# Hybrid diffusion backbone on one Trainium2 core: where the bias of the adaLN conditioning is added

## The reference, cut to what matters

```
mp = adaln(c_ctx[None, :], ada_w[l], ada_b[l])      # (silu(cond) @ w + b).reshape(6, D)
ms = adaln(c, ada_w[l], ada_b[l])
...
ap = modulate(rmsnorm(hp, norm1_g[l]), mp, 0)       # x * (1 + mod[1]) + mod[0]
...
hp = hp + mp[:, 2][:, None, :] * op                 # mod[2]: gate of the mixer
...
hp = hp + mp[:, 5][:, None, :] * hier_moe(modulate(rmsnorm(hp, norm2_g[l]), mp, 3), ...)
```

## Time and profile before

| what | value |
|---|---|
| median of 3 runs | 1781.94 us (1778.7, 1781.94, 1781.96) |
| the profiled execution, its own time | 1779.51 us |
| span of that execution (first to last instruction) | 1777.6 us |
| PE busy | 1667.9 us, 94% of the span |
| DVE, ACT, POOL busy | 606.5, 369.6, 100.1 us |
| DMA | 614.04 MB, mean 345 GB/s |
| line 741 (bias products), PE busy | 12.7 us in 384 records |

### The profile page before, as it was taken

How to read it: one execution, slowest core, us unless ns; L and a number is a source line. 1 busy time by engine, 2 the same in 40 slices (tenths; PEclk the granted TensorE clock), 3 DMA queues, 4 the chain that set the end, 5 groups by cost and what they waited for, 6 DMA issues and landing times.

```text
span 1777.6 us, 20153 instructions
## 1 busy us (share of the span) xinstructions
PE 1667.9 (94%) x8226; PEld 833.1 (47%) x8226; DVE 606.5 (34%) x1327; ACT 369.6 (21%) x705; POOL 100.1 (6%) x158
## 2 busy tenths in 40 slices
PE   5989999899999999899999999988999999999995
PEld 2443333376544333334864433335786654433331
DVE  1142323300532323130176232314333993423233
ACT  2031111110431111120202111112222662311111
POOL 0000000000000000000000000000001960000000
PEclk8999999999999999999999999999999999999998
DMA  9999999996769999998556999998864585899992
GB/s 391 376 423 425 427 425 425 405 365 241 290 243 426 425 426 427 423 373 341 204 194 254 425 425 426 427 423 318 308 237 168 127 268 209 317 418 424 426 425 115
DMA packets 98415, 614.04 MB, mean 345 GB/s; under 512 B 8112, under 2 KB 8384, under 8 KB 52112
## 3 DMA queue, kind: packets, MB, share of 16 engines
q1 hardware_dynamic: 91376, 585.73, 81.0%
q0 software_dynamic: 6944, 26.96, 4.6%
HBM read 608.34 MB, written 4.33 MB: 345 GB/s over the span
## 4 chain that ended last, share of the span: by engine, by line
PE 71%; DMA 14%; DVE 7%; ACT 4%; issue 3%; SPq 0%; POOL 0%; DVEq 0%; POOLq 0%; ACTq 0%
PE psum L1192 20%; PE psum L632 13%; PE psum L1236 10%; PE psum L639 10%; DMA acc<-in_moe_w_down 7%; PE psum L1257 5%; PE psum L733 4%; DMA ring<-in_moe_w_down 3%; PE psum L670 3%; DMA ring<-in_moe_w_up 2%; ACT arena L1603 2%; DMA ring<-in_ada_w 1%; PE psum L1169 1%; DVE arena L2097 1%; ACT arena L1551 1%
## 5 line engine op out<-in xcount | busy, mean ns | idle before, releaser
L1192 PE MATMUL psum<-ring,arena 128*64 128x512 f32 x1152 | 254.2, 597 | 3.5 <-DMA ring<-in_moe_w_up 3.5
L632 PE MATMUL psum<-at,ring 128*128 128x256 f32 x1024 | 225.3, 382 | 3.4 <-ACT at L1389 3.4
L632 PEld LDWEIGHTS psum<-at,ring 128*128 128x128 f32 x1024 | 194.9, 191 | 31.4 <-ACT at L1389 3.5
L639 PE MATMUL psum<-ring,at 128*128 128x512 f32 (+1 forms) x416 | 172.4, 569 | 0.4 <-DVE at L2006 0.4
L1192 PEld LDWEIGHTS psum<-ring,arena 128*64 128x64 f32 x1152 | 81.8, 138 | 161.0 <-issue 161.0
L2158 DVE TENSOR_TENSOR arena<-arena,psum 128x512 f32<-128x512 f32 x32 | 33.7, 1052 | 357.9 <-PE psum L1192 357.9
L1192 PE MATMUL psum<-arena 128*64 128x512 f32 x512 | 142.6, 594 | 0.0
L1236 PE MATMUL psum<-arena 128*64 128x512 f32 x448 | 117.2, 600 | 13.3 <-DMA acc<-in_moe_w_down 8.3
L1257 PE MATMUL psum<-arena 128*128 128x512 f32 x256 | 118.4, 605 | 11.4 <-ACT arena L1603 9.0
L639 PEld LDWEIGHTS psum<-ring,at 128*128 128x128 f32 x416 | 75.2, 190 | 85.9 <-issue 83.5
L1940 DVE COPY_PREDICATED arena<-of_late,psum 128x512 f32<-128x512 int32 x56 | 40.8, 728 | 208.5 <-ACT arena L1596 206.8
(11 more groups left out here) (326 smaller groups left out, 1865.5 us busy)
## 6 DMA issues: line engine op xcount, KB each, us to landing
ring<-in_ada_w SPq DMA_DIRECT2D x48, 2048.0 KB, 13.5
ring<-in_moe_w_gate SPq DMA_DIRECT2D x40, 2048.0 KB, 21.1
ring<-in_moe_w_up SPq DMA_DIRECT2D x32, 2048.0 KB, 19.6
ring<-in_moe_w_down SPq DMA_DIRECT2D x24, 2048.0 KB, 21.9
arena<-in_moe_w_down SPq DMA_DIRECT2D x24, 2048.0 KB, 26.5
arena<-in_moe_w_up SPq DMA_DIRECT2D x16, 2048.0 KB, 17.2
ring<-in_ssd_w_in SPq DMA_DIRECT2D x12, 2048.0 KB, 10.5
arena<-in_moe_w_gate SPq DMA_DIRECT2D x8, 2048.0 KB, 22.8
```

The lines of the kernel that those rows point to most:

```text
L632: last = nc.tensor.matmul(dst, slot(k)[:, c, m * P:(m + 1) * P], src[:, c, :], start=(c == 0), stop=(c == nk - 1))
L639: last = nc.tensor.matmul(dst, src[:, c0 + c, s * P:(s + 1) * P], slot(k)[:, wc0 + c, 0:cols], start=(start and c == 0), stop=(stop and c ...
L1192: last = nc.tensor.matmul(ps[b][e * CAP:(e + 1) * CAP, :], rows, block_rows[:, c, :], start=(h == 0 and c == 0), stop=(h == 1 and c == 3))
```

## The change

`ada_slot` adds the bias only to the groups that hold gate columns: none in round 0, groups 0 and 1 in round 1, groups 2 and 3 in round 2. For the other groups the last weight product closes the accumulation. `modulation` replaces the plain copy of the turned columns by an addition with the bias, which lies in `vecs` as columns already and is broadcast over the two conditionings. `ada_mm` is now raised in rounds 1 and 2 alone, so `ada_evicted` waits for `slot_done` of the last quarter in round 0.

```
-                                                start=(q == 0 and c == 0), stop=False)
+                                                start=(q == 0 and c == 0), stop=(q == QUARTERS - 1 and c == 1 and g not in gates))
                 last.then_inc(slot_done, 1)
-                if q == QUARTERS - 1:
+
+                if q == QUARTERS - 1 and gates:
                     for m in range(4):
-                        for g in range(4):
+                        for g in gates:
...
+                gates = ((), (0, 1), (2, 3))[r]
...
             def ada_evicted(l, r):
-                act.wait_ge(ada_mm, 3 * l + r + 1)
+                if r:
+                    act.wait_ge(ada_mm, 2 * l + r)
+                else:
+                    act.wait_ge(slot_done, AT[max(l - 1, 0) if l != 1 else 1, f"A{l}.0.{QUARTERS - 1}"] + 1)
...
             def modulation(l, r):
-                V.tensor_copy(modt[:, cols, :], bank(6, NMOD * DC, S)[:, cols, :]).then_inc(mod_ready, 1)
+                bias = vec("ada_b")[:, l * NMOD * DC + cols.start:l * NMOD * DC + cols.stop]
+                V.tensor_tensor(modt[:, cols, :], bank(6, NMOD * DC, S)[:, cols, :], bias.unsqueeze(2).to_broadcast([P, cols.stop - cols.start, S]),
+                                ALU.add).then_inc(mod_ready, 1)
```

## The result

| | before | changed kernel |
|---|---|---|
| median of 22 runs each, same chip | 1782.2 us | 1788.86 us |
| lowest and highest | 1778.21, 1788.19 | 1782.46, 1794.37 |
| ratio, 95% interval | 1 | 1.0038 [1.0028, 1.0048] |
| profiled execution: own time, span | 1779.51, 1777.6 | 1788.52, 1786.7 |

A forecast was written before the change was run, and what follows sets the result against it. Expert stages were taken as bound by transfers, mixer stages and borders by PE. 1779.51 - 0.92 - 0.88 + 0.04 = 1777.75 us; the same 1.76 us off the median 1781.94 gave 1780.2 us, range 1776.0 to 1783.5.

The forecast's parts named there:

- Kept: 0.92: Layer 0, round 0, at 30.21 us: removing the bias batch starts the transfer-bound stage up to 318 us 0.92 us earlier.
- Kept: 0.88: Layer 1, round 0, at 351.70 us: removing the bias batch saves 0.88 us ahead of the PE-bound mixer.
- 356.1 that was forecast: Sign in layer 1: products of Q0 should start at 356.1 us instead of 357.8.
- Kept: 0: Layers 2 and 3, round 0, ahead of the experts: removal gains 0; PE only waits 0.9 us longer for a transfer.
- Lost: 0.04: Round 0 of layers 0 and 1: DVE's addition takes 0.02 us more than the copy each, 0.04 us lost.
- The rival that it costs half: Rounds 1 and 2 of layers 1 to 3: halved batches save 0.44 us at six places, 1777.5 us; chance 0.12.
- the estimate of 0.40 us: Halved batches, rounds 1 and 2: at about 60 cycles overhead per matmul, 16 records would need 0.40 us, 32 records 0.80.
- the claim about order: All engines: ACT's place in its order is unchanged, SP and POOL issue the same transfers in order; no added wait.
- a loss has no source here, since nothing is added: Halved batches of rounds 1 and 2: they stay 0.88 us, gain 0, and cannot lose anything.
- The clock's rival: Thinner PE stretches at round 0 make the clock fall more often, 1.76 us each; two or more: 1783.7 us, chance 0.06.
- the forecast's size: Whole kernel: 1.76 us less (0.10%), called "same" with a small gain in it; the forecast had chance 0.70.

The follow-up runs named there:

- Runs 1 and 10: The changed kernel with 64 counting instructions more: ahead of PE's first wait (1780.75 us, ratio 0.9986), or in layer 0's never-run overflow code (1782.13 us, 0.9994).
- run 10: The changed kernel with 64 counting instructions added to layer 0's overflow code, which is never run: 1782.13 us, ratio 0.9994 to the kernel before.
- runs 7 and 8: 32 counting instructions put at the start of the kernel with only rounds 1 and 2 halved (1789.36 us, 1.0034), and of the kernel before (1791.25 us, 1.0045).
- run 9: The kernel before with 64 instructions left out of layer 0's never-run overflow code, nothing executed changed: 1796.29 us against 1783.37, ratio 1.0063.

## Why the prediction was wrong

- **What is executed went as forecast, in part by luck.** "Kept: 0.92" in layer 0: no batch stands between the last quarter and ACT's copy, PE reached 59.34 us for 60.36, SP's issue came at 61.25 for 62.27, and the stage ended 0.96 us earlier. That this total meets the forecast is luck: the last quarter took 3.69 us for 1.92 (granted clock 0.51 over 28 to 32 us for 1.00), and the kernel before lost 1.6 us more between 36 and 41 us (0.72 over 36 to 42 us for 1.00). "Kept: 0.88" in layer 1: between the last quarter of round 0 and Q0, the batch is gone (7.18 us from 350.52 to 357.70, for 7.97 us from 349.85 to 357.82). But Q0 came at 357.70 us and not at the 356.1 that was forecast, because 16 records at 318 us took 1.70 us more at a low clock. "Kept: 0" in layers 2 and 3: PE's wait for `in_moe_w_up` grew to 5.9 us. "Lost: 0.04" for DVE: 181 ns for 180, nothing.
- **The halved batch stays as long as the whole**, 0.86 and 0.90 us in 16 records for 0.88 and 0.92 in 32 at the same places (395 and 462 us). The rival that it costs half falls, and with it the estimate of 0.40 us from the overhead that the Trainium skill gives each matmul ("TensorEngine Tiling (Array Packing)", section "Performance Considerations"). That halved batches are worth nothing either way isn't shown: alone they cost 2.7 and 4.1 us, by a way that stays open.
- **The sum fell at what it left out.** The step that failed is the claim about order: I had compared which instructions stand behind which, found that nothing else on PE moved against its neighbours, and took "a loss has no source here, since nothing is added". The 512 instructions removed (128 products, each two matmul records and two weight loads) move all later code by up to two blocks, and the target of layer 1's jump from 0.09 of a block to 0.84. The missing term is 3.65 and 3.87 us in the two profiles for the stall and 1.76 and 2.68 us for the low clock right behind it, 5.4 and 6.6 us together.
- **The clock's rival was right in kind and too small.** I gave two more falls a chance of 0.06 and tied them to gaps that removed products leave. The profiled execution has five stretches that cost 1.6 to 1.8 us each and have no counterpart before (28, 318, 472, 765 and 1540 us), and the kernel before has two that the changed one lacks (37 and 1190 us). The one at 765 us follows the stall; for the others no cause is shown. Over all runs the mean clock is 0.9826 for 0.984 to 0.985 before, which by the slope is 1.4 to 2.0 us, some of it behind the stall.
- **With the stall away, the forecast's size is there.** Runs 1 and 10 are 3.1 and 1.2 us below their kernels before; 1.8 was forecast, and both intervals hold it (0.9990); that of run 10 holds no gain (1.0000) as well. The changed kernel takes 0.38% more than the kernel before, and the same work with its code at another place 0.06 to 0.14% less.

The account of the median: 1782.2 - 1.8 + 3.7 + 1.8 = 1785.9 us, against 1788.86 measured. Some 3 us are left. Run 10 executes the same instructions and is 0.44% or 7.8 us below the changed kernel by the ratios (5 to 11 by their intervals), so the 3 us may hang on the place of the code as well; by what way isn't shown. Low clock at other places differs between executions, and whether the 2.4 us of the halved batches alone are in the rest is open.

## What to carry to other kernels

Where an engine's program jumps over a long piece of code, any edit ahead of the jump can move its target to a place just behind a block's border, and that was worth up to 4.1 us of stall and 1.4 to 3.0 us of clock behind a long one, more than the edit itself. Before judging an edit of a few instructions, look in the chain and in PE's view in order of time for "issue" pieces of 1 to 4 us at the jumps, and count the targets in blocks of 256 instructions (the border stood at 0.76 of the count here, as the stops of runs 7 and 8 show). If there are such pieces, shift the code by instructions in a branch that never runs, and measure the edit with and without. The version to keep here is the change with its code shifted by 64 instructions (0.9986 and 0.9994 of the kernel before, the second not clear of 1); the shift has to be chosen again after every edit.

## What the runs showed that I had not expected

- A block's fetch that PE waits for from the start costs 3.65 to 4.12 us, while its packet is a single one of 16 KB among the weight transfers. At some jumps only 1.1 to 2.5 us were left to wait.
- With a stall of that length the granted clock falls, and the 32 records behind it take 8.4 to 10.1 us for 7.04. Behind the stall of 1.10 us in run 9 they take 7.10.
- The cost of a semaphore increment on PE, 0.158 us at most, makes padding with it dear where it is executed: 192 of them delayed the first product from 10.91 to 30.27 us.
- Two stalls a few instructions behind the target show the border of a block to the instruction.
